# One more chunk in quarter products: the last chunk of the first feed-forward in a two-block transformer kernel

## The chip, the cores and the metric

The kernel runs on one core of a Trainium2 chip. The metric is the device time of one execution in microseconds (us), launch to end. The core has five engines with queues of their own: TensorE (PE, matrix products into PSUM), VectorE (DVE), ScalarE (ACT), GpSimd (POOL) and SyncE (SP, which only issues DMAs here). They wait for each other on semaphores.

## The reference

Two different transformer blocks run one after the other on 512 tokens with a model width of 1024, all in float32. The part that matters here is the end of the first block and the start of the second:

```python
# first block, end
h2 = rmsnorm(x, norm_mlp_g)
x = x + square(relu(h2 @ w_mlp_in)) @ w_mlp_out      # 1024 -> 4096 -> 1024
y = rmsnorm(x, norm_final_g)
# second block, start: 16 meta tokens in front, then
h = concatenate([meta, y])
z = rmsnorm_2(h, norm_mix) @ w_in                    # first projection of the mixer
```

So when the first feed-forward ends, two sums of squares over the 1024 columns are wanted: that of `x`, and that of `x` times the final gain. Both norms are applied after the product, through `RS`. What the next product needs first is `x` times both gains.

## The kernel before

Activations are kept transposed, as 8 tiles of 128 columns by 512 tokens; `X` is the residual stream. A float32 product is made of three passes over rounded parts: each operand is split in a high part (a copy to fp32r, made by ACT) and a low part (original minus high, made by DVE), and PE computes high x high, high x low, low x high. A *slab* is one output tile over the whole depth: 8 depth tiles x 3 passes = 24 matmuls of 128x512. Its weights are split just ahead of it: `convert(t)` on ACT (`wh`) and DVE (`wl`), two slots that slabs use in turn (`slab % 2`). PE starts slab t when `lo_ready` says that its low weights are there and `evac_done` says that DVE has read the PSUM bank of slab t-2.

A feed-forward works in four chunks of 1024 hidden columns. Each has 8 slabs up (hidden tiles, relu squared), then 8 output tiles that are added to `X`. In the chunks 0 to 2 of both feed-forwards (`strassen_chunk`) the second half goes in four *pairs* of output tiles. Tokens, hidden columns and output columns are each cut in halves, and a pair is made of seven products of quarter blocks and their sums and differences (B11, T1 to T4, B21, B22 of the hidden tiles; A11, A12, A22, S1 to S4 of the weights), 12 matmuls of 128x256 each, instead of eight. Four products go straight to `X`, and what several quarters share is gathered in `mids`. At the end GpSimd adds `mids` to `X` (four operations, `x_combined`). The weight sums S1 and S3 are made by accumulating DMAs that GpSimd issues (`s13_sums`), S2 and S4 by DVE.

The last chunk of the first feed-forward is `mlp_last`, and it is plain: 8 slabs up, 8 slabs down, without quarter products. While its output slabs run, each finished tile m goes through these steps, and the same ones are in the code for all eight:

- DVE: `add_residual` (PSUM to `X`), the low weights of the slab after next, then `Bl[m]`, the low part of the next product's input.
- ACT: the high weights of the slab after next, `square` (`SQ`), a second square with the final gain (`SQ2`), and `Bh[m]`, the high part.
- GpSimd: `SS += SQ` and `SS2 += SQ2` for the tiles 0 to 6. Two buffers each for `SQ` and `SQ2`, so ACT can be two tiles ahead of GpSimd at most. The last tile's additions are DVE's.

After the last tile ACT and DVE split the two sums, and PE multiplies them by ones. PE does this inside the first slab of the second block (`slab_with_stats(T2, ...)`), after depth tiles 0 to 5 and ahead of 6 and 7; each depth tile k waits for `Bl[k]`. Queues are in program order on each engine; nothing reorders them at run time.

Of the kernel before, what the change touches and what calls it, by code (L numbers as in the profile page):

```python
# [23 lines left out]
F32 = mybir.dt.float32  # L24
# [8 lines left out]
P = 128  # L33
# [43 lines left out]
N2_MIX = N_HID + 8  # L77
# [107 lines left out]
def build(nc, d):  # L185
# [24 lines left out]
    with ctx:  # L210
# [7 lines left out]
        X = sb("X", [P, KT, S2])  # L218
        AA, BB = sb("AA", [P, 2, KT, S2], F32R), sb("BB", [P, 2, KT, S2], F32R)
# [94 lines left out]
        SQ2, SS2 = region(8576, 2, S1), region(9600, S2)  # L314
        gain2 = region(10128, KT)
        meta2 = region(10136, KT, META)
        msq = region(10264, KT, META)
# [154 lines left out]
        def so_far(which, per_chunk):  # L472

            return per_chunk * (CHUNKS - 1) if which == REAL else 0
# [58 lines left out]
        HID_END = 12 * 2 * (CHUNKS - 1) + 12  # L533
        PRODUCTS, READS, BASES = 24 * 2 * (CHUNKS - 1), 8 * 2 * (CHUNKS - 1), 32 * 4 * 2 * (CHUNKS - 1)
# [249 lines left out]
        def _(pool):  # L784
# [43 lines left out]
            def strassen_sums(which):  # L828
# [11 lines left out]
                n = 4 if which == REAL else 0  # L840
                pool.tensor_tensor(x[:, :, 0, 1], x[:, :, 0, 1], mids[:, :, 0:HB], ALU.add).then_inc(x_combined, 1)
                pool.tensor_tensor(x[:, :, 1, 0], x[:, :, 1, 0], mids[:, :, 0:HB], ALU.subtract).then_inc(x_combined, 1)
                pool.tensor_tensor(x[:, :, 1, 1], x[:, :, 1, 1], mids[:, :, 0:HB], ALU.subtract).then_inc(x_combined, 1)
                pool.wait_ge(x_combined, n + 3)
                pool.tensor_tensor(x[:, :, 1, 1], x[:, :, 1, 1], mids[:, :, HB:2 * HB], ALU.subtract).then_inc(x_combined, 1)
# [31 lines left out]
            def s13_sums(which, c, q):  # L877
                w = d["w_mlp_out" if which == ONE else "w_ff2_2"][0]
                u = so_far(which, 4) + 4 * c + q
# [35 lines left out]
            pool.memset(k2[:, :, 0:PAD], 0.0)  # L915
            pool.memset(la[:, :, 0:PAD], 0.0)
            pool.memset(v2[:, :, 0:PAD], 0.0)
            after(pool.memset(reset, 1.0))
            pool.memset(reset.rearrange("p (a b) -> p a b", b=CH)[:, :, 0:1], 0.0).then_inc(zeros2_ready, 1)

# [11 lines left out]
            for m in range(KT - 1):  # L932
# [8 lines left out]
                if m == 0:  # L941
                    pool.tensor_copy(SS2[:, META:S2], SQ2[:, 0, :]).then_inc(ss2_done, 1)
                else:
                    pool.wait_ge(ss2_done, m)
                    pool.tensor_tensor(SS2[:, META:S2], SS2[:, META:S2], SQ2[:, m % 2, :], ALU.add)\
                        .then_inc(ss2_done, 1)

# [22 lines left out]
        def _(act):  # L970
# [52 lines left out]
            def strassen_chunk(which, c):  # L1023
                t0, _, p0 = MLPS[which]
                Hh, t = hidden_high(which), t0 + 16 * c
                squares, diffs, fourths = (so_far(which, n) + n * c for n in (8, 8, 4))
                pairs, blocks = so_far(which, 4) + 4 * c, so_far(which, 24) + 24 * c
# [12 lines left out]
                def first_sums(q):  # L1040
                    act.wait_ge(s13_sum[q % 2], 16 * pairs + 32 * (q // 2) + 32)
# [48 lines left out]
                for q in range(4):  # L1090
                    done = blocks + 6 * q
                    if q < 3:
# [8 lines left out]
                    else:  # L1101
                        act.wait_ge(blk_done, done + 5)
                        act.wait_ge(w_landed[p0 % 2], landed_count(p0, 8) + 64 * c)
                        act.activation(w_slab(wh, 0, KT), raw_half(p0 % 2, 0, KT, 2), ACT.Copy).then_inc(hi_ready, 1)
                        act.wait_ge(slab_done, t + 16)
                        act.activation(w_slab(wh, 1, KT), raw_half(p0 % 2, 1, KT, 2), ACT.Copy).then_inc(hi_ready, 1)

            def mlp_last():
                t0, n0, w = T_MLP + 16 * (CHUNKS - 1), N_HID, width(ONE)
                for j in range(16):  # L1110
                    t = t0 + j
                    if j < 7:
                        convert(t + 2)
                    if j < 8:
                        split(n0 + j, Ah[:, j, 0:w], F[:, (n0 + j) % 2, 0:w])
                    else:
                        m = j - 8
                        if m < KT - 1:
                            convert(t + 2)
                        act.wait_ge(evac_done, t + 1)  # L1120
                        square(2, m, ONE)
                        x = X[:, m, META:S2]
                        if m >= 2:
                            act.wait_ge(ss2_done, m - 1)
                        else:
                            act.wait_ge(gain2_ready, 1)
                        act.activation(SQ2[:, m % 2, :], x, ACT.Square, scale=vecT[:, G_FIN + m:G_FIN + m + 1])\
                           .then_inc(sq2_ready, 1)
                        act.activation(Bh[:, m, META:S2], x, ACT.Copy, scale=gain2[:, m:m + 1])\
                           .then_inc(hi_split, 1)  # L1130
                        if m == 0:
                            act.activation(Bh[:, :, 0:META], meta2, ACT.Copy).then_inc(meta_hi, 1)
                    if j == 7:
                        convert(t + 2)
# [1968 lines left out]
```

## Time and profile before

| | |
|---|---|
| median of 3 runs | 1392.55 us (1391.8 to 1393.04) |
| the profiled execution | 1392.7 us, of which its span is 1390.9 us |
| PE busy | 1383.3 us (99% of the span) |
| DVE, ACT, POOL busy | 929.4, 601.2, 212.1 us |
| TensorE clock granted | full speed in all 40 slices |

The span goes from the first to the last instruction. The last chunk of the first feed-forward runs on PE from 656.01 us to 744.98 us: eight slabs up until 700.5 us, eight down after it. The second block's first slab begins at 744.98 us. PE is pipelined, so a matmul's duration in the profile (0.39 us for 512 columns) is longer than the distance to the next one; the pieces of the chain of waits give the true pace.

### The profile page before, as it was taken

The page shows a single profiled execution, that of the slowest core. Times are in us where ns is not written, and L with a number is a line of the kernel's source. Part 1 is how long each engine was busy: PE and PEld are TensorE (multiplying, and loading weights), DVE is VectorE, ACT ScalarE, POOL GpSimd, SP SyncE. Part 2 cuts the span into 40 slices and gives each one's busy share as a digit, 9 for nine tenths or more (in the row PEclk, how much of TensorE's full clock was granted, in tenths as well). Part 3 has the DMA queues.
Part 4 walks back from the last instruction along what each step waited for, and adds up shares of the span by engine and source line. Part 5 has one row for each costly group of instructions (what it writes and reads, how often), then busy time and mean ns, then how long its engine had stood idle before and what let it go on. Part 6 is the DMA issues. An engine that isn't in the chain of part 4 may idle for free.

```text
span 1390.9 us, 21474 instructions
## 1 busy us (share of the span) xinstructions
PE 1383.3 (99%) x8570; PEld 1177.7 (85%) x8570; DVE 929.4 (67%) x1269; ACT 601.2 (43%) x854; POOL 212.1 (15%) x214
## 2 busy tenths in 40 slices
PE   9999999999999999999999999999999999999998
PEld 7887888787888989889888998878888998989886
DVE  6635443766667758587656678656757958758785
ACT  4334532654445344353244445344444525344363
POOL 5000000000032302112332020000022211303310
PEclk9999999999999999999999999999999999999999
DMA  5223123212236936644322222232235763827473
GB/s 188 91 93 113 62 71 109 64 51 72 91 106 157 214 99 169 163 107 135 117 96 76 91 70 77 92 106 88 84 100 139 174 165 99 211 93 203 127 168 119
DMA packets 153003, 161.68 MB, mean 116 GB/s; under 512 B 4106, under 2 KB 140756, under 8 KB 152932
## 3 DMA queue, kind: packets, MB, share of 16 engines
q1 hardware_dynamic: 121012, 129.21, 28.8%
q0 software_dynamic: 31904, 31.46, 12.5%
q8 instruction: 51, 0.84, 0.3%
q14 instruction: 20, 0.16, 0.0%
q10 hardware_dynamic: 16, 0.00, 0.0%
HBM read 157.78 MB, written 2.10 MB: 115 GB/s over the span
## 4 chain that ended last, share of the span: by engine, by line
PE 99%; ACT 0%; issue 0%; DVE 0%; POOL 0%; POOLq 0%; ACTq 0%
PE ps L2465 64%; PE ps L2530 17%; PE ps L2461 4%; PE ps L2487 4%; PE ps L2603 3%; PE ps L2673 1%; PE ps L2891 1%; PE ps L2863 1%; PE ps L2877 1%; PE ps L2983 1%; PE ps L2764 0%; PE ps L3064 0%; PE ps L2807 0%; PE ps L2825 0%; PE ps L2771 0%; PE ps L2589 0%
## 5 line engine op out<-in xcount | busy, mean ns | idle before, releaser
L2465 PE MATMUL ps<-AA,wh 128*128 128x512 f32 x1440 | 454.0, 397 | 0.0
L2465 PE MATMUL ps<-BB,wh 128*128 128x512 f32 x1088 | 341.9, 396 | 0.2 <-issue 0.2
L2465 PEld LDWEIGHTS ps<-AA,wh 128*128 128x128 f32 x1440 | 268.1, 188 | 65.4 <-issue 2.9
L2465 PE MATMUL ps<-AA,wl 128*128 128x512 f32 x720 | 283.7, 394 | 0.0
L985 ACT ACTIVATE wh<-raw 128x1024 fp32r<-128x1024 f32 (+2 forms) x149 | 141.5, 950 | 253.7 <-PE ps L2465 203.5
L2465 PEld LDWEIGHTS ps<-BB,wh 128*128 128x128 f32 x1088 | 202.8, 188 | 49.2 <-issue 1.8
L1536 DVE TENSOR_TENSOR wl<-raw,wh 128x1024 fp32r<-128x1024 f32 (+2 forms) x149 | 170.4, 1143 | 69.5 <-ACT wh L985 69.2
L2465 PE MATMUL ps<-BB,wl 128*128 128x512 f32 x544 | 214.1, 394 | 0.0
L2465 PEld LDWEIGHTS ps<-AA,wl 128*128 128x128 f32 x720 | 135.7, 188 | 30.7
L2465 PEld LDWEIGHTS ps<-BB,wl 128*128 128x128 f32 x544 | 102.5, 188 | 23.1
L2530 PE MATMUL ps<-Hl,wh 128*128 128x256 f32 x384 | 108.6, 283 | 0.0
L1613 DVE TENSOR_TENSOR wl<-raw,wh 128x1024 fp32r<-128x1024 f32 x48 | 62.3, 1297 | 30.2 <-ACT wh L1033 15.1
L2530 PE MATMUL ps<-Hl,Sh 128*128 128x256 f32 x288 | 81.2, 282 | 0.0
L1581 DVE TENSOR_TENSOR arena<-ps,RS 128x512 f32<-128x512 f32 (+1 forms) x54 | 37.4, 692 | 65.0 <-PE ps L2465 61.6
L2530 PEld LDWEIGHTS ps<-Hl,wh 128*128 128x128 f32 x384 | 72.7, 189 | 0.0
L1033 ACT ACTIVATE wh<-raw 128x1024 fp32r<-128x1024 f32 x36 | 38.2, 1061 | 65.7 <-PE ps L2465 65.7
L1675 DVE SCALAR_TENSOR_TENSOR zf<-ps,RS 128x512 f32<-128x512 f32 x48 | 33.2, 692 | 45.9 <-PE ps L2465 45.2
L2530 PE MATMUL ps<-BB,wh 128*128 128x256 f32 x192 | 54.7, 285 | 0.0
L2530 PEld LDWEIGHTS ps<-Hl,Sh 128*128 128x128 f32 x288 | 54.3, 188 | 0.2
L2530 PE MATMUL ps<-AA,wh 128*128 128x256 f32 x192 | 54.3, 283 | 0.0
L2530 PE MATMUL ps<-BB,wl 128*128 128x256 f32 x192 | 53.9, 281 | 0.0
L2530 PE MATMUL ps<-AA,wl 128*128 128x256 f32 x192 | 53.9, 281 | 0.0
(417 smaller groups left out, 2380.0 us busy)
## 6 DMA issues: line engine op xcount, KB each, us to landing
raw<-in_w_in SPq DMA_DIRECT2D x38, 1024.0 KB, 5.5
raw<-in_w_ff SPq DMA_DIRECT2D x31, 1024.0 KB, 5.4
raw<-in_w_mlp_in SPq DMA_DIRECT2D x16, 1024.0 KB, 5.4
raw<-in_w_mlp_out SPq DMA_DIRECT2D x16, 1024.0 KB, 4.8
zf<-in_w_mlp_out POOLq DMA_DIRECT2D x48, 256.0 KB, 4.7
zf<-in_w_ff POOLq DMA_DIRECT2D x48, 256.0 KB, 4.4
raw<-in_w_out SPq DMA_DIRECT2D x8, 1024.0 KB, 4.8
arena<-in_x SPq DMA_DIRECT2D x4, 512.0 KB, 6.8
```

Source lines behind the costliest of these rows:

```text
L985: act.activation(w_slab(wh, t % 2, kt), raw_slab(t), ACT.Copy).then_inc(hi_ready, 1)
L1033: act.activation(w_slab(wh, j % 2, KT), raw_half((p0 + i) % 2, j % 2, KT, 2), ACT.Copy)\
L1536: dve.tensor_tensor(w_slab(wl, t % 2, kt), raw_slab(t), w_slab(wh, t % 2, kt), ALU.subtract)\
L1581: dve.tensor_tensor(tokens(dst, kind), dense_psum(t, kind)[0:rows], tokens(scale, kind), ALU.mult)\
L1613: dve.tensor_tensor(w_slab(wl, slot, KT), raw_half(p % 2, slot, KT, 2), w_slab(wh, slot, KT), ALU.subtract).then_inc(lo_ready, 1)
L1675: dve.scalar_tensor_tensor(out=f, in0=halves(dense_psum(t0 + j, which)), scalar=0.0, in1=halves(RS[:, 0:S1]), op0=ALU.max, op1=ALU.mult).t ...
L2461: last = pe.matmul(dense_psum(t_ps, ALL)[:, half, :], a[:, k, :], b[:, o0 + k, half * HALF2:(half + 1) * HALF2], start=start, stop=stop)
L2465: last = pe.matmul(dense_psum(t_ps, kind), a[:, k, :], b[:, o0 + k, col0:col0 + S1], start=start, stop=stop)
L2487: mm = pe.matmul(value_part(t, a), x[:, k, of], w[:, k - k0, :], start=(k == 0 and i == 0 and not (narrow and a % 2)), stop=(k == KT - 1 a ...
L2530: mm = pe.matmul(ps[:, bank, 0:HB], w[:, k, :], hidden_part(x, k, b), start=(first and k == 0 and i == 0), stop=(k == 3 and i == 2), skip_ ...
L2603: mm = pe.matmul(ps[:, bank, :], x, v[:, k, :], start=(first and k == 0 and n == 0), stop=(k == 3 and n == 2), skip_group_check=True)
L2673: return pe.matmul(dense_psum(t, ONE), w_slab(w, t, KT)[:, k, :], x[:, k, 0:S1], start=first, stop=last)
```

## The change

The last chunk of the first feed-forward is now made by `strassen_chunk` as well, with `n_pairs=2`. Its hidden tiles are kept in halves and sums (in `Hh` and `Hl`), output tiles 0 to 3 are two pairs of seven quarter products, and output tiles 4 to 7 stay plain slabs. These read the same hidden storage: the lower depth tiles from B21 and B22, the upper ones from B11 and the place behind it, where T1 stood. For that, B12 is copied behind B11 during the second pair (`behind_left`: one ACT copy of 128x1024 and one DVE subtraction).

GpSimd now adds `mids` to `X` for pairs 2 and 3 only, at the start of the chunk. For the pairs 0 and 1 DVE does it after the second pair, in three operations. Only then are the tiles 0 to 3 final, and squares, splits and sums of all four follow at once, ahead of and between those of tiles 4 to 7. The sums' buffers move (`SQ2` to `F`, `SS2` behind the hidden tiles in `AA`, gains and meta tokens to the arena's end), and GpSimd's memsets for the second block move from the chunk's start to behind its sums.

```diff
+        LAST_PAIRS = 2
@@ GpSimd
+                else:
+                    for q in range(LAST_PAIRS):
+                        s13_sums(which, CHUNKS - 1, q)
                 pool.wait_ge(evac_done, t0 + 16 * (CHUNKS - 1))
-                x = X[:, :, META:S2].rearrange("p (q o) (t n) -> p q o t n", o=2, t=2)
+                q0, n = (0, COMBINED) if which == REAL else (LAST_PAIRS, 0)
+                x = X[:, 2 * q0:KT, META:S2].rearrange("p (q o) (t n) -> p q o t n", o=2, t=2)
...
@@ ACT, mlp_last
+                strassen_chunk(ONE, CHUNKS - 1, LAST_PAIRS)
+                for m in range(KT):
+                    if m == 0:
+                        act.wait_ge(x_combined, COMBINED)
+                        act.wait_ge(gain2_ready, 1)
+                    if LAST_PAIRS == 2 and m == 2:
+                        convert(t0 + 14)
+                    elif 2 * LAST_PAIRS + LAST_PAIRS // 2 <= m < KT - 1:
+                        convert(t0 + 10 + m)
+                    if m >= 2 * LAST_PAIRS:
+                        act.wait_ge(evac_done, t0 + 8 + m + 1)
+                    square(2, m, ONE)
...
@@ DVE, mlp_last
+                strassen_chunk(ONE, CHUNKS - 1, LAST_PAIRS)
...
+                dve.tensor_tensor(x[:, :, 0, 1], x[:, :, 0, 1], u, ALU.add).then_inc(x_combined, 1)
+                dve.tensor_tensor(x[:, :, 1], x[:, :, 1], u.unsqueeze(2).to_broadcast([P, LAST_PAIRS, 2, HB]),
+                                  ALU.subtract).then_inc(x_combined, 1)
+                dve.wait_ge(x_combined, COMBINED - 1)
+                dve.tensor_tensor(x[:, :, 1, 1], x[:, :, 1, 1], v, ALU.subtract).then_inc(x_combined, 1)
...
+                normed_low(0)
...
+                normed_low(1)
+                for m in range(2 * LAST_PAIRS, KT):
+                    t = t0 + 8 + m
+                    add_residual(t, t, m, ONE)
+                    if m < KT - 1:
                         convert(t + 2)
+                    if LAST_PAIRS == 2 and m == 4:
+                        normed_low(2)
+                        normed_low(3)
...
+                    normed_low(m)
@@ PE, mlp_last
-                for j in range(1, 16):
-                    ops = HIDDEN[ONE] if j >= 8 else NORMED[ONE]
-                    full_slab(t0 + j, *ops, 0, ONE, split_ready(N_HID) if j == 8 else None)
+                strassen_chunk(ONE, CHUNKS - 1, LAST_PAIRS)
+                first_plain = 8 + 2 * LAST_PAIRS
+                for j in range(first_plain, 16):
+                    t = t0 + j
+                    h, l = w_slab(wh, t % 2, KT), w_slab(wl, t % 2, KT)
+                    pe.wait_ge(lo_ready, t + 1)
+                    pe.wait_ge(mid_read, FIRST_MLP["reads"])
+                    pe.wait_ge(evac_done, t0 + first_plain - 2 if j == first_plain else t - 1)
...
+                    for k in range(KT):
+                        x = [hidden_part(part, k % 4, B11 if k < 4 else B21, 2) for part in (Hh, Hl)]
```

The order on VectorE before, in the middle of the last chunk's output slabs. `X<-X,ps` is `add_residual`, `wl<-raw,wh` the low weights, `BB<-X,arena,BB` is `Bl` of one tile:

```order
L1601 TENSOR_TENSOR X<-X,ps 128x512
L1536 TENSOR_TENSOR wl<-raw,wh 128x1024
L1773 SCALAR_TENSOR_TENSOR BB<-X,arena,BB 128x512
L1601 TENSOR_TENSOR X<-X,ps 128x512
L1536 TENSOR_TENSOR wl<-raw,wh 128x1024
L1773 SCALAR_TENSOR_TENSOR BB<-X,arena,BB 128x512
```

And now, from the end of the second pair until the residual of output tile 5. The first `X<-X,ps` is the second pair's, the next ones those of tiles 4 and 5:

```order
L1768 TENSOR_TENSOR X<-X,ps 128x256
L1640 TENSOR_TENSOR wl<-raw,wh 128x1024
L1782 TENSOR_TENSOR X<-X,zf 128x2x256
L1783 TENSOR_TENSOR X<-X,zf 128x2x512
L1786 TENSOR_TENSOR X<-X,zf 128x2x256
L1790 SCALAR_TENSOR_TENSOR BB<-X,arena,BB 128x512
L1796 TENSOR_TENSOR BB<-arena,BB 128x8x16
L1790 SCALAR_TENSOR_TENSOR BB<-X,arena,BB 128x512
L1628 TENSOR_TENSOR X<-X,ps 128x512
L1563 TENSOR_TENSOR wl<-raw,wh 128x1024
L1790 SCALAR_TENSOR_TENSOR BB<-X,arena,BB 128x512 x3
L1628 TENSOR_TENSOR X<-X,ps 128x512
```

Three additions over `mids` (`zf`) stand ahead of everything that tiles 0 to 3 want, and four extra `Bl` operations stand ahead of the residual of tile 5.

The order on ScalarE now, from the weights of output slab 5 on (`SQ<-X` is the square, `F<-X,vecT` the second one, `BB<-X,arena` is `Bh`):

```order
L1136 ACTIVATE wh<-raw 128x1024
L1024 ACTIVATE SQ<-X 128x512
L1155 ACTIVATE F<-X,vecT 128x512
L1157 ACTIVATE BB<-X,arena 128x512
L1160 ACTIVATE BB<-arena 128x8x16
L1024 ACTIVATE SQ<-X 128x512
L1155 ACTIVATE F<-X,vecT 128x512
L1157 ACTIVATE BB<-X,arena 128x512
L1011 ACTIVATE wh<-raw 128x1024
L1024 ACTIVATE SQ<-X 128x512
L1155 ACTIVATE F<-X,vecT 128x512
L1157 ACTIVATE BB<-X,arena 128x512
```

Before, one `wh<-raw` stood ahead of each tile's three operations. Now the weights of output slab 6 stand behind tiles 0 and 1, and those of output slab 7 behind tiles 2, 3 and 4.

## Rows read from the trace of the kernel before

**Rows 1.** The page, busy time; then windows with busy time, clock, DMA share.

```profile
PE 1383.3 (99%) x8570; PEld 1177.7 (85%) x8570; DVE 929.4 (67%) x1269; ACT 601.2 (43%) x854; POOL 212.1 (15%) x214
...
656.01:700.50 44.49, 44.49 (x193) 36.07 (x193) 29.48 (x31) 12.69 (x15) 15.46 (x15) 1.00 0.29 95
700.50:744.98 44.48, 44.48 (x195) 36.12 (x194) 25.03 (x26) 21.44 (x31) 22.70 (x14) 1.00 0.26 83
...
1298.91:1343.41 44.50, 44.50 (x193) 35.93 (x193) 34.87 (x42) 21.62 (x28) 15.86 (x8) 1.00 0.43 120
```

**Rows 2.** The chain that ended last, pieces in time: start, us, what.

```profile
616.09 39.92 PE ps L2530 x336
656.01 88.97 PE ps L2465 x384
744.98 4.37 PE ps L2461 x36
```

**Rows 3.** Timeline of DVE, end of chunk 1's last pair: start, us, operation.

```profile
569.98 1.23 DVE L1613 TENSOR_TENSOR wl<-raw,wh 128x1024 fp32r<-128x1024 f32 x1 [1.91 <-ACT wh L1104]
571.13 0.68 DVE L1734 TENSOR_TENSOR X<-X,ps 128x512 f32<-128x512 f32 x1
571.72 0.42 DVE L1738 TENSOR_TENSOR X<-X,ps 128x256 f32<-128x256 f32 x1
572.73 1.22 DVE L1613 TENSOR_TENSOR wl<-raw,wh 128x1024 fp32r<-128x1024 f32 x1 [0.59 <-ACT wh L1106]
```

**Rows 4.** Timeline of ACT, the steps of output tile 2.

```profile
717.28 1.06 ACT L985 ACTIVATE wh<-raw 128x1024 fp32r<-128x1024 f32 x1 [2.81 <-PE ps L2465]
718.24 0.62 ACT L998 ACTIVATE SQ<-X 128x512 f32<-128x512 f32 x1
718.77 0.71 ACT L1127 ACTIVATE arena<-X,vecT 128x512 f32<-128x512 f32 x1
719.38 0.71 ACT L1129 ACTIVATE BB<-X,arena 128x512 fp32r<-128x512 f32 x1
```

**Rows 5.** Timeline of POOL, output tiles 0 (copies), 2 and 6.

```profile
708.90 0.60 POOL L942 COPY arena<-arena 128x512 f32<-128x512 f32 x1
...
718.94 1.81 POOL L939 TENSOR_TENSOR SS<-SS,SQ 128x512 f32<-128x512 f32 x1 [2.11 <-ACT SQ L998]
720.72 1.74 POOL L945 TENSOR_TENSOR arena<-arena 128x512 f32<-128x512 f32 x1
...
742.96 1.74 POOL L945 TENSOR_TENSOR arena<-arena 128x512 f32<-128x512 f32 x1
```

**Rows 6.** Timeline of DVE, the steps of output tile 2.

```profile
717.22 0.69 DVE L1601 TENSOR_TENSOR X<-X,ps 128x512 f32<-128x512 f32 x1 [1.54 <-PE ps L2465]
718.37 1.23 DVE L1536 TENSOR_TENSOR wl<-raw,wh 128x1024 fp32r<-128x1024 f32 x1 [0.46 <-ACT wh L985]
720.12 1.18 DVE L1773 SCALAR_TENSOR_TENSOR BB<-X,arena,BB 128x512 fp32r<-128x512 f32 x1 [0.52 <-ACT BB L1129]
```

**Rows 7.** Timeline of POOL at the chunk's start: two of four additions to `X`.

```profile
656.62 2.39 POOL L841 TENSOR_TENSOR X<-X,zf 128x1024 f32<-128x1024 f32 x1 [22.50 <-DVE X L1738]
658.98 3.39 POOL L842 TENSOR_TENSOR X<-X,zf 128x1024 f32<-128x1024 f32 x1
...
664.80 3.26 POOL L845 TENSOR_TENSOR X<-X,zf 128x1024 f32<-128x1024 f32 x1
```

**Rows 8.** Timeline of DVE beside them.

```profile
657.14 2.96 DVE L1613 TENSOR_TENSOR wl<-raw,wh 128x1024 fp32r<-128x1024 f32 x1 [0.60 <-ACT wh L1106]
...
665.72 0.68 DVE L1753 TENSOR_TENSOR F<-ps,RS 128x512 f32<-128x512 f32 x1
```

**Rows 9.** Timeline of DVE at the end of the first block.

```profile
746.40 0.69 DVE L1548 TENSOR_TENSOR SS<-SS,SQ 128x512 f32<-128x512 f32 x1 [0.70 <-ACT SQ L998]
```

**Rows 10.** Timeline of PE: the two sums, then the first slab again.

```profile
749.34 0.50 PE L2931 MATMUL ps<-AA,ones 128*128 128x512 f32 x1
...
750.65 0.74 PE L2461 MATMUL ps<-BB,wh 128*128 128x264 f32 x4
```

More of the change, by code:

```diff
@@ L470, in hidden_part, with so_far, first_sums_landed, behind_left @@
             return t[:, k, b * HB:(b + n) * HB]
-        def so_far(which, per_chunk):
-            return per_chunk * (CHUNKS - 1) if which == REAL else 0
+        LAST_PAIRS = 2
+        FIRST_MLP = {"squares": 8 * CHUNKS, "fourths": 4 * CHUNKS, "parts": 12 * CHUNKS + 1, "second": CHUNKS,
+                     "pairs": 4 * (CHUNKS - 1) + LAST_PAIRS, "blocks": 24 * (CHUNKS - 1) + 6 * LAST_PAIRS,
+                     "reads": 8 * (CHUNKS - 1) + 2 * LAST_PAIRS}
+        COMBINED = 4 + 3
+        def so_far(which, what):
+            return FIRST_MLP[what] if which == REAL else 0
+        def first_sums_landed(which, c, q):
+            before = 2 * (CHUNKS - 1) + (LAST_PAIRS + 1 - q % 2) // 2 if which == REAL else 0
+            return 32 * (before + q // 2 + 1) + 64 * c
+        upper_right = zf[:, 5632:7680].rearrange("p (s n) -> p s n", s=4)[:, ::-1, 0:HB]
+        def behind_left(t):
+            return t[:, :, T1 * HB:(T1 + 1) * HB]
         def quarter(p, o, kappa):
@@ L878, in s13_sums @@
                 w = d["w_mlp_out" if which == ONE else "w_ff2_2"][0]
-                u = so_far(which, 4) + 4 * c + q
+                u = so_far(which, "pairs") + 4 * c + q
                 S3, S1_ = third(q), first(q)
@@ L1021, in gate, with strassen_chunk @@
                                scale=0.5).then_inc(gate_done, 1)
-            def strassen_chunk(which, c):
+            def strassen_chunk(which, c, n_pairs=4):
                 t0, _, p0 = MLPS[which]
                 Hh, t = hidden_high(which), t0 + 16 * c
-                squares, diffs, fourths = (so_far(which, n) + n * c for n in (8, 8, 4))
-                pairs, blocks = so_far(which, 4) + 4 * c, so_far(which, 24) + 24 * c
+                diffs, fourths = so_far(which, "squares") + 8 * c, so_far(which, "fourths") + 4 * c
+                pairs, blocks = so_far(which, "pairs") + 4 * c, so_far(which, "blocks") + 24 * c
                 def slab_weights(j):
@@ L1089, in strassen_chunk @@
                         lower(0)
-                for q in range(4):
+                for q in range(n_pairs):
                     done = blocks + 6 * q
-                    if q < 3:
+                    if q < n_pairs - 1:
                         act.wait_ge(blk_done, done + 1)
@@ L1108, in mlp_last @@
             def mlp_last():
[L1109 to L1134, printed above, removed]
@@ L1602, in add_residual, with strassen_chunk @@
                    .then_inc(evac_done, 1)
-            def strassen_chunk(which, c):
+            def strassen_chunk(which, c, n_pairs=4):
                 t0, _, p0 = MLPS[which]
                 Hh, t = hidden_high(which), t0 + 16 * c
-                squares, parts = so_far(which, 8) + 8 * c, so_far(which, 12) + 12 * c
-                pairs, blocks = so_far(which, 4) + 4 * c, so_far(which, 24) + 24 * c
-                reads = so_far(which, 8) + 8 * c
+                squares, parts = so_far(which, "squares") + 8 * c, so_far(which, "parts") + 12 * c
+                pairs, blocks = so_far(which, "pairs") + 4 * c, so_far(which, "blocks") + 24 * c
+                reads = so_far(which, "reads") + 8 * c
                 def slab_weights(p, slot, count):
@@ L1714, in strassen_chunk @@
                         lower(0)
-                for q in range(4):
+                for q in range(n_pairs):
                     g1, g2, g3, g4 = pair_banks(q)
-                    done, last = blocks + 6 * q, q == 3
+                    done, last = blocks + 6 * q, q == n_pairs - 1
                     x0, x1 = X[:, 2 * q, META:S2], X[:, 2 * q + 1, META:META + HB]
@@ L2538, in strassen_chunk @@
                     products(t0 + j, j % 2, KT, *NORMED[which], 0, which, 0, KT).then_inc(slab_done, 1)
-                for q in range(4):
+                for q in range(n_pairs):
                     g1, g2, g3, g4 = pair_banks(q)
@@ L2551, in strassen_chunk @@
                     if q == 0:
-                        pe.wait_ge(s2_lo, so_far(which, 1) + c + 1)
+                        pe.wait_ge(s2_lo, so_far(which, "second") + c + 1)
                         pe.wait_ge(evac_done, t + 8)
```

161 lines of the change are left out of this document (88 added, 73 removed).

## The prediction

> **What bounds the kernel now.** I read the page's busy times and the clock first: PE is busy 1383.3 of 1390.9 us at full clock [rows 1]. So the time is what PE has to do plus the few gaps between. Next the chain of waits, for PE's pace: the chunk that changes is one piece of 384 matmuls in 88.97 us without a gap, or 231.7 ns for one of 512 columns; a chunk's four pairs are 336 matmuls in 39.92 us, or 118.8 ns for one of 256 columns [rows 2]. Third, the windows: the stretch of the eight output slabs is all PE, with DVE busy 25.0, ACT 21.4 and GpSimd 22.7 of 44.48 us [rows 1]. These three look idle, but their work hangs on tiles that come 5.56 us apart (24 x 231.7 ns). The change lets four tiles come at once, so I read the timelines of the three, step by step, and then the handover to the second block: PE does 4.37 us of its first slab [rows 2], goes straight on to the sums at 749.34 and is back in the slab at 750.65 [rows 10], 5.67 us after the last output slab. There is no slack there: whatever makes the sums later makes PE later.
>
> **What PE saves.** Four slabs go: 96 x 231.7 ns = 22.24 us. Two pairs come: 168 x 118.8 ns = 19.96 us. Gain 2.3 us. The four plain slabs that stay have the same matmuls. The full gain is thus below 0.2% of the time.
>
> **What is hidden in the chunk's first part.** The up slabs now carry the longer hidden-tile work. The second feed-forward's last chunk has the same, with four GpSimd additions of 128x1024 running beside it, and its eight slabs take 44.50 us, no gap [rows 1]. Here GpSimd has four additions of half that size. I take 0, also for the two more groups of weight sums: their DMAs go out during chunk 2, as those of the chunks before do. Inside the second pair B12 is copied behind B11. ACT can do it after the second of seven products (2.9 us into the pair) and DVE, after its `mids` read at 6.4 us, needs about 1.2 us (a two-input operation of 1024 columns is 1.22 to 1.23 us [rows 3]); the next weights come from ACT only later. At such a pair's end the low weights are ready at 571.21, 0.39 us before PE wants them (pair's end: 571.60) [rows 3]. I take 0; unhidden it is at most these 1.2 us.
>
> **What waits at the end.** Clock zero is the end of the second pair on PE. If nothing waits, four slabs end at 22.24, and PE is back from the sums at 22.24 + 5.67 = 27.9.
>
> DVE first. The low weights of slab 5 end at 2.35, as 573.95 does after 571.60 [rows 3]. Then the three additions of `mids`: 128x512, 128x1024, 128x512, at 0.69 [rows 9], 1.25 and 0.69, the third waiting for the first two. `X` is whole at 4.9. ACT then squares tile 0 and needs 0.53 + 0.61 + 0.61 = 1.75 us a tile by its starts [rows 4], GpSimd starts at 5.6.
>
> GpSimd's price per addition. The rows say 1.81 and 1.74 us [rows 5], but part of that is waiting. At 656.62 GpSimd adds for 2.39 us, and the DVE subtraction that began at 657.14 ends 2.96 us later, where one alone takes 1.23; the next GpSimd addition takes 3.39 us and ends 2.27 us after DVE's end (662.37 against 660.10) [rows 7, 8, 3]. So the two take turns, one whole operation at a time. A DVE operation with an input in PSUM doesn't join in: 0.68 us in the middle of such an addition [rows 7, 8]. With turns, tile 2 comes out: DVE's weights end at 719.60, GpSimd's addition at 720.7, DVE's `Bl` at 721.30, GpSimd's second at 722.46 [rows 5, 6]. That is 1.15 us for an addition of 512 columns, 0.66 for `Bl`, 1.14 for low weights.
>
> The page "SBUF — State Buffer" of the Trainium skill, section "Who interferes with whom", has the same rule: GpSimd and a DVE operation with two inputs in SBUF share ports under an exclusive lock, and the loser blocks for the whole instruction. It speaks against this change; without that rule, tiles that come at once would cost little, which is the first rival below. "Perfetto Trace Analysis" of the Trainium skill, section "GPSIMD Engine Instruction", says to time GpSimd by the spacing of starts and not by reported durations. By the reported 1.81 and 1.74 us with DVE's turns on top, the twelve additions would come out 7.5 us longer (12 x 0.63).
>
> Now the queue. GpSimd has from 5.6 on: two copies at 0.60 and twelve additions at 1.15 = 15.0 us. DVE takes a turn between them for seven `Bl` at 0.66, three low weights at 1.14 and the meta tiles' 0.2, together 8.2 us. GpSimd's last addition (tile 6) thus ends at 5.6 + 15.0 + 8.2 = 28.8. DVE's addition of tile 7 needs it, and also its turn. From that operation's start to PE's return it is 746.40 to 750.65, 4.25 us [rows 9, 10]. PE is back at 33.1 instead of 27.9: **5.2 us of waiting**.
>
> On the way there PE waits in three places, which are parts of these 5.2 us and not added to them. First, slab 6: ACT makes its high weights behind tiles 0 and 1, at 9.7; DVE gets the port at 10.6 and ends at 11.85, where PE wanted them at 11.12: 0.8 us. Second, slab 7: ACT's second square of tile 4 needs the buffer that GpSimd frees by adding tile 2, at 14.8. `Bh` of tile 4 ends at 16.1, the high weights at 17.1, DVE has `Bl` of tile 4 and the residual of tile 5 before the low weights, and these end at 19.6 after another GpSimd turn; PE was free at 17.45: 2.2 us. Slab 7 ends at 25.2, six depth tiles of the next slab at 29.5. Third, the sums: 2.2 us.
>
> GpSimd's additions without a DVE turn between start 2.36 us apart for 1024 columns instead of 2.27 [rows 7]: 0.09 more. A few such places, and its slower answer to a new square, I estimate at 0.2 us together.
>
> **Sum.** -2.3 + 5.2 + 0.2 = +3.1 us. The profiled execution took 1392.7 us (its span and 1.8 around it), 0.15 above the median of 1392.55. From the span: 1390.9 + 3.1 = 1394.0 for the new one, 1395.8 with what lies around, and against the median 1395.6, which is my forecast. Nothing takes it back later: what follows the sums (scales, reciprocal, second block) hangs on them at the same distances as before, and PE is the bound there too. GpSimd's memsets, now behind its sums, are over about 1.4 us later, before DVE asks for them.
>
> Bounds. An addition at 1.0 us makes +1.2, one at 1.3 us makes +4.8.
>
> **Rivals.**
> 1. The end waits hardly at all, because the turns cost less than I read or GpSimd catches up. Without any turns GpSimd has its 15.0 us done by 20.6 and then only waits for tile 6 (22.7), only slab 7 waits, for 0.9 us: -2.3 + 0.9 = -1.4, 1391.1 us. For it: all three engines are under 60% busy there. Against it: rows 7 and 8. This is the one on the other side: it decides if GpSimd's last addition ends before about 25.
> 2. No wait at all, the pure gain: -2.3, 1390.2 us. Against it speaks already that tiles 0 to 3 are complete only at 4.9.
> 3. GpSimd wins every tie for the port. Then low weights wait for whole strings of additions: slab 6's come only near 18.8, and the sum is +5.5, 1398.1 us. Against it: at tile 2 DVE got its turn between the two additions [rows 5, 6].
> 4. The forecast, and in addition the second pair or the copy of B12 is late: +1.2 more, 1396.8 us. For it: only 0.39 us of slack [rows 3].
>
> **How the numbers follow.** Forecast 0.65 (its own range 1394.3 to 1397), rival 1 0.14, rival 2 0.05, rival 3 0.08, rival 4 0.08. The range of 1393.2 to 1398.2 leaves out the first two rivals and holds the bounds of GpSimd's price but for the lowest. 0.2% is 2.8 us, about what a measurement of this kernel can tell from no change, and the forecast of +3.1 lies close to it: two thirds of its chance are above. Slower by over 0.2%: 0.43 + 0.08 + 0.08, so 0.60. Faster by over 0.2% would need more than PE's whole gain: 0.02. Within: 0.38.
>
> **What would show it.** In the new profile: two pairs in 19.9 to 20.0 us and no gap before their end; the three `X<-X,zf` on DVE ending about 4.9 us after the pairs; a back-to-back GpSimd queue from 5.6 to about 29; PE gaps of about 0.8 ahead of slab 6, 2.2 ahead of slab 7, 2.2 at the sums; DVE's weight subtractions longer than 1.23 us. Wrong: GpSimd done before 25, no gap ahead of slab 7, or gaps ahead of the first plain slab or inside the pairs.

## The result, and the profile after

The changed kernel takes 1395.05 us (median of 19 runs, 1394.16 to 1396.57), the kernel before, on the same chip, 1392.49 us (median of 19, 1391.8 to 1394.53). The ratio is 1.0017, with a 95% interval of 1.0011 to 1.0024: slower by 0.17%, or by 2.56 us between the medians. My forecast was 1395.6, with a range of 1393.2 to 1398.2.

The profiled execution took 1394.16 us, the lowest of the kernel's runs (the kernel before: 1392.7). The page of the changed kernel, its busy line, to be held against the first row of [rows 1]:

```profile
PE 1381.0 (99%) x8642; PEld 1177.8 (85%) x8642; DVE 942.6 (68%) x1298; ACT 613.6 (44%) x872; POOL 215.9 (16%) x222
```

PE does 2.3 us less, as the arithmetic of matmuls promised (1383.3 to 1381.0), and the kernel is slower all the same. So the loss must be idle time of PE, which is small beside 99% and easily missed on this line. The next view shows it: what PE waited for, over the whole changed kernel (its first two rows: us in total, times, longest us).

```profile
PE ps L2625 <- DVE wl L1563: 2.1, 2, 1.5
PE ps L2979 <- DVE AA L1820: 1.8, 1, 1.8
```

Both rows are new: the same view of the kernel before starts with 1.7 us for `ident`, which both kernels have, and holds nothing from this stretch. L2625 is the plain output slab, L2979 the first matmul of the sums. PE's timeline has their places (start us, us, operation, and in brackets the idle time ahead of it with its releaser), and the chain the pieces around them:

```profile
732.35 0.50 PE L2625 MATMUL ps<-AA,wh 128*128 128x512 f32 x1 [0.62 <-DVE wl L1563]
739.69 0.50 PE L2625 MATMUL ps<-AA,wh 128*128 128x512 f32 x1 [1.50 <-DVE wl L1563]
751.71 0.50 PE L2979 MATMUL ps<-AA,ones 128*128 128x512 f32 x1 [1.83 <-DVE AA L1820]
```

```profile
656.25 44.49 PE ps L2498 x192
700.74 19.88 PE ps L2563 x168
...
753.17 7.40 PE ps L2494 x60
```

The up slabs take 44.49 us with no gap, as before [rows 1, 2]. The two pairs take 19.88 us. From the pairs' end (720.62) PE would be back in the next slab at 748.68 if nothing waited (22.24 for four slabs and 5.82, the distance from 744.98 to 750.80 of the kernel before, by the chain). It is back at 753.17: 4.5 us of waiting. From the chunk's start to PE's return it is 96.92 us, where before it was 94.79 (656.01 to 750.80). The change costs 2.13 us here: 2.36 gained, 4.5 waited. The two profiled executions are only 1.46 us apart, because the first trace of the changed kernel was quicker elsewhere: in the chunks 0 to 2 of both feed-forwards, four pairs took 39.92 us in five of six chunks before and in one of six after, and 39.66 to 39.68 in the others, 0.94 us less in all.

Why the three waits exist is read on GpSimd. Its timeline, from its first copy (5.6 us after the pairs) to its last addition, which ends 28.3 us after them:

```profile
726.22 0.61 POOL L955 COPY SS<-SQ 128x512 f32<-128x512 f32 x1 [59.49 <-ACT SQ L1024]
726.78 0.61 POOL L961 COPY AA_plain<-F 128x512 f32<-128x512 f32 x1
728.12 1.35 POOL L958 TENSOR_TENSOR SS<-SS,SQ 128x512 f32<-128x512 f32 x1 [0.73 <-ACT SQ L1024]
...
735.11 1.75 POOL L958 TENSOR_TENSOR SS<-SS,SQ 128x512 f32<-128x512 f32 x1
736.82 1.74 POOL L964 TENSOR_TENSOR AA_plain<-AA_plain,F 128x512 f32<-128x512 f32 x1
738.52 2.27 POOL L958 TENSOR_TENSOR SS<-SS,SQ 128x512 f32<-128x512 f32 x1
740.74 1.75 POOL L964 TENSOR_TENSOR AA_plain<-AA_plain,F 128x512 f32<-128x512 f32 x1
...
747.65 1.29 POOL L964 TENSOR_TENSOR AA_plain<-AA_plain,F 128x512 f32<-128x512 f32 x1
```

Behind the third row, no row has an idle time in brackets (the rows left out have none either): it never catches up. The starts lie 1.70 us apart where DVE has one operation of 512 columns with two SBUF inputs in between (735.11, 736.82, 738.52), and 2.22 where it has the weights' subtraction of 1024 columns (738.52 to 740.74). DVE pays the same way. Its two weight subtractions in question, and its addition of the sums, which has to wait for GpSimd's:

```profile
730.57 1.73 DVE L1563 TENSOR_TENSOR wl<-raw,wh 128x1024 fp32r<-128x1024 f32 x1
...
737.93 1.71 DVE L1563 TENSOR_TENSOR wl<-raw,wh 128x1024 fp32r<-128x1024 f32 x1
...
747.80 1.69 DVE L1575 TENSOR_TENSOR SS<-SS,SQ 128x512 f32<-128x512 f32 x1 [1.56 <-POOL SS L958]
```

The subtraction was 1.23 alone [rows 6]. The addition was 0.69 [rows 9] and is 1.69 behind 1.56 of idling. The last piece is ACT, whose square for the next tile waits for the buffer that GpSimd frees; the weights of slab 7 stand behind it:

```profile
735.18 0.72 ACT L1155 ACTIVATE F<-X,vecT 128x512 f32<-128x512 f32 x1 [0.95 <-POOL AA_plain L964]
...
736.43 1.04 ACT L1011 ACTIVATE wh<-raw 128x1024 fp32r<-128x1024 f32 x1
```

The chain of waits that ended last says the same of the sums. From 726.22 to 747.75 its pieces are GpSimd's operations and nothing else (the time of each is split over its line and `issue`), and from there it goes over DVE to the first matmul of the sums:

```profile
746.40 1.31 POOL SS L958
747.75 0.04 issue
747.80 1.19 DVE SS L1575
...
751.71 0.50 PE ps L2979
```

### The profile page after: what moved, and what is told of

The parts are those of the page before. It is cut to its first block, busy times and chain, and to the rows that moved or that the text cites. A ratio compares the mean times of both kernels' runs of the same rounds, so it can differ in the third digit from the quotient of the medians.

```text
span 1392.4 us, 21693 instructions
## 1 busy us (share of the span) xinstructions
PE 1381.0 (99%) x8642; PEld 1177.8 (85%) x8642; DVE 942.6 (68%) x1298; ACT 613.6 (44%) x872; POOL 215.9 (16%) x222
## 4 chain that ended last, share of the span: by engine, by line
PE 97%; issue 1%; DVE 0%; POOL 0%; ACT 0%; POOLq 0%; ACTq 0%; DVEq 0%
PE ps L2498 60%; PE ps L2563 19%; PE ps L2520 4%; PE ps L2494 4%; PE ps L2651 3%; PE ps L2721 1%; PE ps L2939 1%; PE ps L2911 1%; PE ps L2925 1%; PE ps L3031 1%; PE ps L2812 0%; PE ps L3112 0%; PE ps L2855 0%; PE ps L2698 0%; PE ps L2873 0%
## 5 line engine op out<-in xcount | busy, mean ns | idle before, releaser
L2498 PE MATMUL ps<-AA,wh 128*128 128x512 f32 x1312 | 413.6, 397 | 0.0
L2498 PEld LDWEIGHTS ps<-AA,wh 128*128 128x128 f32 x1312 | 243.6, 188 | 60.1 <-issue 2.9
L2498 PE MATMUL ps<-AA,wl 128*128 128x512 f32 x656 | 258.2, 394 | 0.0
L1011 ACT ACTIVATE wh<-raw 128x1024 fp32r<-128x1024 f32 (+2 forms) x137 | 128.9, 941 | 225.6 <-PE ps L2498 175.4
L1563 DVE TENSOR_TENSOR wl<-raw,wh 128x1024 fp32r<-128x1024 f32 (+2 forms) x137 | 155.1, 1132 | 57.4 <-ACT wh L1011 57.1
L2498 PEld LDWEIGHTS ps<-AA,wl 128*128 128x128 f32 x656 | 123.4, 188 | 28.3
L2563 PE MATMUL ps<-Hl,wh 128*128 128x256 f32 x416 | 116.5, 280 | 0.0
L1640 DVE TENSOR_TENSOR wl<-raw,wh 128x1024 fp32r<-128x1024 f32 x56 | 71.0, 1267 | 33.5 <-ACT wh L1059 17.2
L2563 PE MATMUL ps<-AA,wh 128*128 128x256 f32 x224 | 62.9, 281 | 0.0
L2563 PE MATMUL ps<-AA,wl 128*128 128x256 f32 x224 | 62.7, 280 | 0.0
```

What stands on the lines that cost most here:

```text
L1011: act.activation(w_slab(wh, t % 2, kt), raw_slab(t), ACT.Copy).then_inc(hi_ready, 1)
L1563: dve.tensor_tensor(w_slab(wl, t % 2, kt), raw_slab(t), w_slab(wh, t % 2, kt), ALU.subtract)\
L1640: dve.tensor_tensor(w_slab(wl, slot, KT), raw_half(p % 2, slot, KT, 2), w_slab(wh, slot, KT), ALU.subtract).then_inc(lo_ready, 1)
L2498: last = pe.matmul(dense_psum(t_ps, kind), a[:, k, :], b[:, o0 + k, col0:col0 + S1], start=start, stop=stop)
L2563: mm = pe.matmul(ps[:, bank, 0:HB], w[:, k, :], hidden_part(x, k, b), start=(first and k == 0 and i == 0), stop=(k == 3 and i == 2), skip_ ...
```

## The experiments

The theory: GpSimd's additions and DVE's operations with two inputs in SBUF go in turns (one waits while the other works), so GpSimd's queue of fourteen operations ends late, and this makes all three waits. If so, PE's 2.4 us gain appears when the turns go. The rivals: the late completion of tiles 0 to 3 (4.8 us after the pairs) would make PE wait anyhow, or the place of the weights in the order does. Each timed kernel ran 11 times, with the kernel before on the same chip: e1 to e4 on one (median of the kernel before 1393.46, 33 runs), e5 to e7 on another (1392.45, 27 runs). e8 to e10 are one profiled execution each. Between kernels I compare by ratio, and by the time from the output slabs' start to PE's return: 50.30 us for the kernel before (700.50 to 750.80) and 52.43 for the changed one (700.74 to 753.17).

**e1, the additions become writes.** The squares are not added up, so the two sums are left out of the result.

```diff
-                    pool.tensor_tensor(SS[:, 0:S1], SS[:, 0:S1], SQ[:, f % 2, 0:S1], ALU.add).then_inc(ss_done, 1)
+                    after(pool.memset(SS[:, 0:S1], 1.0))
+                    pool.memset(SS[:, 0:S1], 1.0).then_inc(ss_done, 1)
...
-                    pool.tensor_tensor(SS2[:, META:S2], SS2[:, META:S2], SQ2[:, m % 2, :], ALU.add)\
+                    after(pool.memset(SS2[:, META:S2], 1.0))
+                    pool.memset(SS2[:, META:S2], 1.0).then_inc(ss2_done, 1)
```

> The changed kernel, but GpSimd's twelve additions of tiles 1 to 6 (SS and SS2) are each replaced by two memsets of 128x512 into the same buffer: about the same time on GpSimd (a memset of 128x576 takes 0.58 us, so some 1.1 to 1.2 us for two), but nothing is read. The sums are left out by this. Theory (turns at the port that both read through): DVE's operations go back to 0.75 and 1.23 us, GpSimd is done by about 23 us after the pairs instead of 28.3, PE waits 0.8 to 1.2 us instead of 4.4, so some 3.3 us less than the changed kernel, 1.0 to 1.5 below the kernel before. Rival (GpSimd is simply too slow for four tiles at once, whatever DVE does): its queue is as long as before, less at most the few tenths between memset and addition, and the time stays within 1 us of the changed kernel.

Measured: 1391.9 us (1390.82 to 1392.41), ratio 0.9988 [0.9979, 0.9997]. GpSimd has nearly the same amount to do per tile (two memsets of 0.53 us, 1.05 us by the starts, for an addition that takes 1.28 where DVE has no turn), but it only writes. Its rows beside DVE's subtraction and at the end, DVE's and the waits of PE in e1 (its lines are one further down):

```profile
730.44 0.53 POOL L958 MEMSET SS<- 128x512 f32 x1 [0.53 <-ACT SQ L1025]
731.02 0.52 POOL L959 MEMSET SS<- 128x512 f32 x1
...
742.13 0.53 POOL L966 MEMSET AA_plain<- 128x512 f32 x1
```

```profile
730.21 1.22 DVE L1564 TENSOR_TENSOR wl<-raw,wh 128x1024 fp32r<-128x1024 f32 x1
```

```profile
PE ps L2626 <- DVE wl L1564: 0.4, 1, 0.4
```

The subtraction is back at 1.22, GpSimd is done 22.4 us after the pairs instead of 28.3, the wait at the sums is gone, and of the two at the slabs 0.4 is left. It takes 49.03 us to PE's return (700.29 to 749.32). The twelve replacements are 2.8 us shorter than twelve additions without a turn, but GpSimd now idles 2.0 us behind its first one, waiting for squares, so I estimate that at most 0.8 of the 5.9 us comes from the shorter work. It is thus not GpSimd's amount of work that costs, but that its additions shut out DVE, and DVE them. The time is 1.56 us below the kernel before by the medians and 1.27 in the stretch; the theory had 1.0 to 1.5.

**e2, the additions cut to 16 columns.** GpSimd adds only 16 of the 512 columns, in both sums (the edit of `SS2` is alike); the rest is left out of the result.

```diff
-                    pool.tensor_tensor(SS[:, 0:S1], SS[:, 0:S1], SQ[:, f % 2, 0:S1], ALU.add).then_inc(ss_done, 1)
+                    pool.tensor_tensor(SS[:, 0:16], SS[:, 0:16], SQ[:, f % 2, 0:16], ALU.add).then_inc(ss_done, 1)
```

> The changed kernel with GpSimd's twelve additions cut to 16 of 512 columns (the other columns' sums are left out). Both the theory of turns and the rival of a slow GpSimd expect the waits ahead of slab 7 and of the sums to go, and only some 0.8 us to stay: 1.0 to 1.5 us below the kernel before, 3.3 to 3.8 below the changed one. If the wait came from ScalarE or VectorE having four tiles at once, or from the later finish of tiles 0 to 3 by itself, it would stay, and the time would be within 1 us of the changed kernel.

Measured: 1391.67 us (1391.14 to 1392.31), ratio 0.9986 [0.9977, 0.9995]. From e2's timeline of GpSimd, two additions that have one and the same amount to do:

```profile
728.76 0.26 POOL L958 TENSOR_TENSOR SS<-SS,SQ 128x16 f32<-128x16 f32 x1 [0.73 <-ACT SQ L1024]
...
731.45 1.05 POOL L958 TENSOR_TENSOR SS<-SS,SQ 128x16 f32<-128x16 f32 x1 [1.86 <-ACT SQ L1024]
```

```profile
731.20 1.22 DVE L1563 TENSOR_TENSOR wl<-raw,wh 128x1024 fp32r<-128x1024 f32 x1
```

The second began while DVE's weight subtraction ran, and ended with it (732.50 and 732.42): a reported duration four times as long, and what is added to it is waiting. That is a turn in a single pair of rows. To PE's return it takes 48.94 us (701.38 to 750.32), 1.36 less than the kernel before (1.79 by the medians, where both views expected 1.0 to 1.5). The four slabs take 1.0 us more than their 22.24. So with the turns nearly gone there is still a remainder of about 1 us, ahead of slab 7: it is what my first rival had as 0.9, with its sum of -1.4. It comes from tiles 0 to 3 coming late. In e2 the chain of waits doesn't touch GpSimd; it goes from DVE's last addition of `mids` (725.37) over ACT's steps of tiles 0 to 4 and the weights of slab 6, one behind another, and over DVE to slab 7:

```profile
735.48 0.62 ACT BB L1157
...
737.48 1.15 DVE wl L1563
738.62 0.04 issue
738.67 5.84 PE ps L2625 x24
```


**e3, the weights of slab 7 one tile earlier.**

```diff
-                    elif 2 * LAST_PAIRS + LAST_PAIRS // 2 <= m < KT - 1:
+                    elif m == 4:
+                        convert(t0 + 15)
+                    elif m == 6:
```

> The changed kernel with the weights of output slab 7 split one tile earlier on ScalarE and VectorE, ahead of tile 4's squares. Theory (GpSimd's last addition sets the end, the other waits lie inside its time): the 1.7 us ahead of slab 7 shrink or move to the sums, and the total stays within 1 us of the changed kernel (2 to 3.5 us above the kernel before). Rival (each wait of PE counts by itself): 1.7 us less than the changed kernel, under 1 us above the kernel before.

Measured: 1395.62 us (1395.2 to 1396.27), ratio 1.0014 [1.0005, 1.0023]. What PE waits for in e3 (its lines are three further down):

```profile
PE ps L2628 <- DVE X L1630: 2.2, 1, 2.2
...
PE ps L2982 <- DVE AA L1823: 1.2, 1, 1.2
PE ps L2628 <- DVE wl L1565: 0.6, 1, 0.6
```

The wait for slab 7's weights is gone, and one of 2.2 us has come for DVE's residual addition, which is now behind those weights in DVE's order. The sum is 4.0 us where it was 3.9, and it takes 52.66 us to PE's return. GpSimd's last addition ends 28.3 us after the pairs, as without the edit. The order isn't the cause: the three waits are one backlog, and to move work within it only changes where it comes out.

**e4, the first pair finished early.** GpSimd adds `mids` of pair 0 while the second pair runs, ACT squares tile 0 then, and tile 1 right after the pair; DVE adds only pair 1.

```diff
+            pool.wait_ge(mid_read, FIRST_MLP["reads"] - 2)
+            xa, xb = X[:, 0, META:S2], X[:, 1, META:S2]
+            pool.tensor_tensor(xa[:, HB:S1], xa[:, HB:S1], mids[:, 0, 0:HB], ALU.add).then_inc(x_combined, 1)
...
-                x = X[:, 0:2 * LAST_PAIRS, META:S2].rearrange("p (q o) (t n) -> p q o t n", o=2, t=2)
+                x = X[:, 2:4, META:S2].rearrange("p (q o) (t n) -> p q o t n", o=2, t=2)
```

> The changed kernel with the first pair finished early: GpSimd adds mids to tiles 0 and 1 while the second pair runs on PE, ScalarE squares tile 0 ahead of the pair's end and tile 1 just behind it, DVE adds mids for tiles 2 and 3 only. GpSimd's queue then starts 7 us earlier, at about -1 instead of 5.6, with two tiles instead of four at once. Theory: GpSimd no longer sets the end, PE waits 0 to 1 us in all, and the time is 1.3 to 2.3 us below the kernel before. Rival (what costs is DVE's and ScalarE's work around the pairs, which this pushes into the tight end of the second pair): a new gap of 1 to 3 us ahead of the first plain slab, and no gain over the kernel before.

Measured: 1392.31 us (1391.32 to 1393.94), ratio 0.9993 [0.9984, 1.0002]. The additions keep their full width, but the first four of GpSimd's fourteen operations are over 5.0 us after the pairs, before the changed kernel's first one starts (5.6). PE waits 0.5 and 0.6 us in e4 (`PE ps L2640`, `L2994`):

```profile
PE ps L2994 <- DVE AA L1835: 0.6, 1, 0.6
PE ps L2640 <- DVE wl L1578: 0.5, 1, 0.5
```

It takes 49.30 us to PE's return (701.51 to 750.81), 3.1 less than the changed kernel. The turns stay and most of the waiting goes: 1.4 us of it is left, of 4.5 (by starts, 49.30 less the 47.94 of no wait). That is more than the 0 to 1 us that I expected, and the median is 1.15 us below the kernel before, where I had 1.3 to 2.3; the rival's gap ahead of the first plain slab did not come. What matters is when GpSimd's queue may start.

**e5, the changed kernel again,** unaltered, beside e6 and e7.

> The changed kernel once more, as a control on the chip that the next three share, and for a second trace. The waits of PE behind the pairs depend on fixed sequences and should come out within 0.3 us of the 4.4 us of the first trace. If the first profiled execution was a lucky one only outside the changed chunk, its time differs in the pace of the quarter products (39.7 or 39.9 us for four pairs) and not in these waits. Time: 2 to 3 us above the kernel before.

Measured: 1395.95 us (1394.02 to 1396.4), ratio 1.0021 [1.0012, 1.0030]. The waits of PE are those of the first trace, and from the slabs' start to PE's return it is 52.43 us again. But the profiled execution took 1396.34 us, 2.18 more than the first, and the pace of the quarter products, which I had named for such a difference, makes the smaller part of it. Where the rest went is below, with e8 to e10.

**e6, one pair instead of two.**

```diff
-        LAST_PAIRS = 2
+        LAST_PAIRS = 1
```

> The changed kernel with one pair instead of two (output tiles 2 to 7 plain). PE's gain halves to 1.15 us. Theory (a queue on GpSimd that four tiles at once make longer than the rest of the slabs can work off): with two tiles at once and six slabs behind them GpSimd has caught up before the last one, PE waits 0 to 0.3 us, and the time is 0.8 to 1.2 us below the kernel before. Rival (a fixed price for finishing any tiles late): half the gain with most of the loss, 1 to 3 us above the kernel before.

Measured: 1391.35 us (1390.79 to 1391.93), ratio 0.9992 [0.9983, 1.0001]. PE has no wait in this stretch, and it takes 49.20 us to its return (700.65 to 749.85). That is 1.10 less than the kernel before, and one pair's whole gain is 1.16 (48 slab matmuls at 231.7 ns less 9.96 us). In e6's timeline of GpSimd idle times of over 1 us appear from the fifth tile on:

```profile
729.08 1.81 POOL L958 TENSOR_TENSOR SS<-SS,SQ 128x512 f32<-128x512 f32 x1 [1.05 <-ACT SQ L1024]
...
734.58 1.82 POOL L958 TENSOR_TENSOR SS<-SS,SQ 128x512 f32<-128x512 f32 x1 [1.99 <-ACT SQ L1024]
```

Two tiles come at once, six more slabs follow at 5.56 us each, and GpSimd catches up.

**e7, as e4, and the first two squares added straight into the sum,** without the two copies.

```diff
-                if m == 0:
-                    pool.tensor_copy(SS[:, 0:S1], SQ[:, f % 2, 0:S1]).then_inc(ss_done, 1)
-                else:
+                if m == 1:
+                    pool.tensor_tensor(SS[:, 0:S1], SQ[:, 0, 0:S1], SQ[:, 1, 0:S1], ALU.add).then_inc(ss_done, 2)
+                elif m > 1:
```

> The kernel with the first pair finished early, and GpSimd adds the squares of tiles 0 and 1 in one operation each instead of copying tile 0's first: two operations of 0.6 us fewer in its queue (for each sum). Theory: GpSimd ends 1.1 us earlier, which takes 0.3 to 0.8 us of the waits that the early pair still has (1.5 us of gaps): 1.4 to 2.1 us below the kernel before. If the rest of the waits are not GpSimd's, it stays at the early pair's time, 1.1 below.

Measured: 1391.48 us (1391.15 to 1393.72), ratio 0.9994 [0.9985, 1.0003]. From the slabs' start to PE's return it is 49.32 us, against 49.30 in e4. I had expected less, and missed (the ratio to the kernel before is e4's too, 0.9994 and 0.9993): in e4 the copies lie ahead of the burst, while GpSimd would else be idle, and without them the first addition has to wait for tile 1. In both kernels the addition for tile 2 starts 27.18 us after the output slabs' start, behind 2.29 us of idling. The waits of PE are 0.5 and 0.6 us as in e4. Two operations were saved that cost nothing.

**e8 to e10, the changed kernel three times more,** one profiled execution each, to find what makes 1394.2 in some executions and 1396.3 in others.

> The changed kernel unaltered, one profiled execution. Theory (the clock makes the slower half of its times): if this execution takes 1395.5 us or more, TensorE's granted clock is near 0.5 for some 3 us right behind the gaps at the sums, and the 60 matmuls of the slab take about 9.0 us; at 1394.8 or less they take 7.4. Rival (the pace of the quarter products in the other chunks, 39.66 or 39.92 us for four pairs, makes it): the 60 matmuls take 7.4 us either way, and the chunks add up to the difference. The three waits of PE are the same 4 to 4.5 us in both.

> As the run before: the changed kernel unaltered. Clock theory: 9.0 us for the 60 matmuls at 1395.5 us or more, 7.4 us at 1394.8 or less. Pace rival: 7.4 us either way.

> As the two runs before: the changed kernel unaltered. Clock theory: 9.0 us for the 60 matmuls at 1395.5 us or more, 7.4 us at 1394.8 or less. Pace rival: 7.4 us either way.

Measured: 1395.85, 1396.4 and 1395.65 us. e9 can be laid on the first trace, since its pairs start at 700.78 and those of the first trace at 700.74. The windows of e9, and then of the first trace (busy time with its count for PE, PEld, DVE, ACT and POOL; granted clock; DMA share; GB/s):

```profile
752.00:753.00 1.00, 1.00 (x6) 0.61 (x5) 1.00 (x2) 0.00 (x0) 0.00 (x0) 0.94 0.00 0
753.00:756.00 3.00, 3.00 (x16) 3.00 (x15) 2.23 (x5) 0.00 (x0) 0.00 (x0) 0.50 0.42 84
756.00:757.00 1.00, 1.00 (x9) 1.00 (x9) 0.10 (x1) 0.76 (x2) 0.00 (x0) 0.85 1.07 381
```

```profile
753.00:756.00 3.00, 3.00 (x27) 3.00 (x26) 2.69 (x6) 1.17 (x3) 0.00 (x0) 1.00 0.38 83
```

```profile
753.30 8.82 PE ps L2494 x60
```

In e9 the granted clock is 0.50 (1.2 GHz) from 753 to 756, right behind the three gaps, and back at 1.00 after 757. PE is busy all the time but 16 matmuls fall in these 3 us instead of 27, and the 60 matmuls take 8.82 us instead of 7.40. In the five traces of the changed kernel they take 7.40 us (execution of 1394.16), 8.88 (1395.65), 8.24 (1395.85), 8.97 (1396.34) and 8.82 (1396.4). In e8 the clock is 0.62 already between 752 and 753, so part of its loss is in the sums: 53.08 us from the slabs' start to PE's return. With such parts counted, and without the 0.09 by which some traces have slower pairs, the clock cost 1.4 to 1.6 us in each of the four. None of the three new executions took 1394.8 us or less, so the lower half of the theory rests on the first trace alone, and e8's 8.24 us misses the 9.0 of the upper half. The traces of the kernel before, e1, e2, e4, e6 and e7, with at most 1.1 us of waiting there, have 7.40 or 7.41. e3 has the long gaps and had 7.41 in its one trace. But the mean granted clock that is on record for every run speaks for more than these traces: 0.998, the lowest value, stands in 12 of the 30 timed runs of the changed kernel, all of 1395.0 us or more, and in 4 of e3's 11, and in none of the 55 of e1, e2, e4, e6 and e7 or the 60 of the kernel before beside them. A short fall can be missed by this mean: e8 and e9 have 0.999 and fell. The rival has a part too: in e9 the three chunks of the second feed-forward have four pairs in 39.92 us each, in the first trace in 39.68. Of the 2.24 us between the two executions this makes 0.72 and the clock 1.42; PE's return is 0.13 later.

## Why the prediction was right, and where not

- PE's gain: 2.3 forecast, 2.36 in the trace (19.88 us for the pairs instead of 19.96), and 2.3 on the page's busy line.
- The chunk's first part and the inside of the pairs: taken as hidden, and hidden: 44.49 us, no wait in 168 matmuls. Rival 4 fell, by little. The low weights for the first plain slab were ready at 720.14, with PE due at 720.62 (start 718.91, 1.23 us).
- DVE's three additions of `mids`: whole at 4.9 us forecast, 4.8 measured (725.42 less 720.62). GpSimd's start at 5.6: measured 5.6.
- The turns: forecast from [rows 5 to 8]. e1 and e2 show that they are the cause, by taking them away in two different ways. Of the 4.5 us of waiting 1.0 is left in e2 and 1.1 in e1 (49.03 less the 47.94 of no wait, which is 19.88 + 22.24 + 5.82). Rival 1, no turns, is thus not what happens, but its figure of -1.4 is what e2 measured (-1.36). Rivals 2 and 3 fell: there are waits, and GpSimd does not win strings of turns; DVE has a turn in nine of the eleven places between its twelve additions.
- The size: the waiting was forecast at 5.2 + 0.2 and is 4.5. The mis-sized terms are the turns and the additions, and their errors have opposite signs. From the first addition of GpSimd to the end of its last I had 22.0 us (12 x 1.15 + 8.2); it is 20.8 (728.12 to 748.94). An addition without a turn takes about 1.28 us by the starts, not 1.15, which is 1.6 us more in twelve. The turns come to about 5.5 us and not 8.2: there are nine instead of ten, and they add 0.43 and 0.94 us (1.71 and 2.22 by the starts, less 1.28) where I had 0.66 and 1.14. That the sum of the two came out within 1.2 us is in part luck. With my price of a turn and the right one of an addition I would have forecast +4.7 (3.1 + 12 x 0.13), near the upper of my bounds.
- GpSimd also idled 0.73 us for tile 1's square, which I had only as part of the 0.2. Together its end is at 28.3 instead of 28.8 (1.2 less and 0.7 more). The rest of the 0.9 is that 0.2, counted apart, and 0.15 between the two readings of how long PE takes to its return (5.67 by the timeline, 5.82 by the chain). The 1.15 came from one place, where the borders of the operations had to be guessed. The spacing of starts in a full queue gives it directly, but [rows 5] had no full queue.
- The rule of the Trainium skill ("SBUF — State Buffer", section "Who interferes with whom") that the loser blocks for the whole instruction agrees with these runs: the 16-column addition of e2 took 0.8 us longer beside a subtraction that it came 0.25 us behind. Only the length is a little shorter than the rule lets expect: by their starts in e1 DVE's operations take 0.67 and 1.15 us, and a turn adds 0.43 and 0.94 to GpSimd's spacing, so about 0.2 us of each overlap. Which part of the operations this is, no run shows.
- The three places: 0.8, 2.2 and 2.2 forecast. By starts they are 0.8, 1.7 and 2.0 (0.62, 1.50 and 1.83 of idling by the records). e3 shows that they are one backlog, as I had counted them.
- "Nothing takes it back later, at the same distances as before" was wrong as a step, though not by the turns. The gaps themselves can cost more afterwards: in four of five traces the clock fell behind them, at a cost of 1.4 to 1.6 us. I hadn't looked at what a gap does to the granted clock, because the kernel before has it at 1.0 throughout this stretch [rows 1].
- The sum: +3.1 forecast, +2.13 in the stretch of the first trace, +2.56 between medians. The nearness of 1395.05 to 1395.6 is in part two errors against each other: 0.9 too much waiting, and a clock loss of up to 1.6 in part of the executions that was not in it. I had given 0.60 to more than 0.2%, and the ratio is at 0.17% with 0.2% inside its interval, so the likelier side by my chances was not the one that was measured. One reading of my own bounds was wrong too: the lower one, +1.2, gives 1393.75 us, and the range of 1393.2 to 1398.2 does hold it.

No version was shown to beat the kernel before by more than its interval. e4, e6 and e7 (the whole computation, medians 1.0 to 1.2 us below that of the kernel before on the same chip) touch 1 with theirs. All three are clearly faster than the changed one: their intervals end at 1.0003 at most, and those of the changed kernel begin at 1.0011. What stays open is why the clock fell behind the same gaps in four traces of the changed kernel and not in the fifth, nor in e3's, and what exactly about the gaps does it: no run changed them one at a time.

## What to carry to other kernels

When a change makes work come in a burst instead of spread out, look at the engine behind it whose operations are slow and serial, and price its queue by the spacing of starts, with every operation of another engine that it takes turns with. Less work for the engine that bounds the kernel is worth nothing if its helpers' backlog ends after it: here one pair kept nearly its whole gain (1.10 of 1.16 us in its stretch) and two lost it. And moving an item within a backlog moves the wait, it doesn't shorten it; letting the queue start earlier does.

## What the runs showed of the hardware

- A GpSimd addition of 512 columns and a DVE operation with two SBUF inputs exclude each other for whole operations, but for about 0.2 us: additions start 1.28 us apart alone, 1.71 with a DVE operation of 512 columns in between and 2.22 with one of 1024. A 16-column addition took 1.05 us instead of 0.26 beside a DVE subtraction of 1024 columns (e2). GpSimd's memsets do not shut DVE out (e1: 1.22 us beside memsets of 0.53).
- The granted clock fell from 1.0 to 0.5 for about 3 us behind gaps of 0.8, 1.7 and 2.0 us (by the starts of matmuls) that lie within 20 us, in four of five traced executions with the same gaps. It cost 1.4 to 1.6 us, nearly as much as one of the longer gaps. In e3's one trace it stayed at 1.0 behind like gaps, and it did so in all traces whose gaps here were recorded as 0.6 us at most.
- 336 matmuls of 256 columns take 39.92 or 39.66 to 39.68 us (118.8 or 118.1 ns each), at a clock of 1.0, and change between the two from chunk to chunk and from execution to execution of one kernel. With six such groups this alone makes up to 1.4 us between two executions.
